# Holding the next weight slabs until the input tiles are in, copying the rotary tables across partitions on GpSimd, and three smaller edits in a hybrid encoder layer

## The reference

```python
h = rms_norm(x, norm_mix_pre)
u_pool, q, k, v, g_pool, g_attn = split(h @ w_in)          # 512, 1536, 1536, 1536, 1024, 1024
y_pool = pool_mixer(u_pool, w_pool_grp, pool_scale) @ w_pool_br   # 4 groups, centred means minus self
q, k = apply_rope(q, cos, sin), apply_rope(k, cos, sin)
o, lse = dilated_window_attention(q, k, v, dilation, 64)   # 3 head groups: dilation 1, 4, 16
y_attn = merge(o, lse) @ w_attn_br
x = x + rms_norm((sigmoid(g_pool) * y_pool + sigmoid(g_attn) * y_attn) @ w_out, norm_mix_post)
h2 = rms_norm(x, norm_ffn_pre)
x = x + rms_norm((silu(h2 @ w_ffn_gate) * (h2 @ w_ffn_up)) @ w_ffn_down, norm_ffn_post)
```

## Time and profile before

| | us |
|---|---|
| median of 3 runs (lowest, highest) | 1183.47 (1183.24, 1185.29) |
| the profiled execution | 1180.95 |
| its span on the slowest core | 1179.4 |
| spans of the other cores | 1174.4 to 1179.4 |
| PE busy in the span | 1086.2 (92%) |
| DVE, ACT, POOL busy | 538.1, 461.7, 86.3 |

### The profile page before, as it was taken

One profiled execution on the slowest core, in us unless ns is written; L12 is line 12 of the kernel. 1 busy time (PEld: TensorE's weight loads), 2 busy tenths in 40 slices (PEclk: granted clock), 3 DMA queues, 4 the chain that ended last, 5 costly groups with the idle time before them and its releaser, 6 DMA issues.

```text
span 1179.4 us, 19451 instructions; the slowest of 8 cores (1174.4 to 1179.4 us)
## 1 busy us (share of the span) xinstructions
PE 1086.2 (92%) x6781; PEld 591.4 (50%) x6896; DVE 538.1 (46%) x823; ACT 461.7 (39%) x882; POOL 86.3 (7%) x173
## 2 busy tenths in 40 slices
PE   2689989799999899999999999999999999999995
PEld 1456746455776487444444444444444444444442
DVE  3464485796548867334434867412121221222331
ACT  3453455565555555622222877411111111112211
POOL 6210000000000000001000000111111010000000
PEclk9799999999999999999999999999999999999998
DMA  8951210112021302623301842355544220333321
GB/s 190 229 135 28 37 28 11 19 21 44 10 43 22 64 11 38 126 39 57 49 1 54 262 151 106 54 82 83 82 76 73 36 36 1 108 108 107 108 90 54
DMA packets 32399, 84.62 MB, mean 72 GB/s; under 512 B 4016, under 2 KB 4272, under 8 KB 32176
## 3 DMA queue, kind: packets, MB, share of 16 engines
q0 software_dynamic: 18768, 36.31, 19.8%
q1 hardware_dynamic: 13536, 47.06, 12.2%
HBM read 102.89 MB, written 16.78 MB: 101 GB/s over the span
## 4 chain that ended last, share of the span: by engine, by line
PE 77%; DVE 7%; ACT 6%; DMA 5%; issue 4%; ACTq 0%; DVEq 0%; SPq 0%; POOL 0%; POOLq 0%
PE ps L173 64%; PE ps L170 12%; DMA arena<-x 5%; ACT arena L184 5%; DVE arena L187 2%; DVE arena L190 2%; DVE arena L201 2%; ACT arena L255 0%; DVE arena L197 0%; DVE ps L187 0%; DVE arena L195 0%; PE ps L176 0%; ACTq L68 0%; DVEq L68 0%; ACT L255 0%
## 5 line engine op out<-in xcount | busy, mean ns | idle before, releaser
L173 PE MATMUL ps<-arena 128*128 128x512 bf16 (+2 forms) x4196 | 916.2, 368 | 26.9 <-DVE arena L201 15.5
L173 PEld LDWEIGHTS ps<-arena 128*128 128x128 bf16 x4304 | 410.9, 98 | 487.6 <-issue 39.3
L184 ACT ACTIVATE arena<-ps 128x512 bf16<-128x512 f32 (+5 forms) x556 | 339.6, 619 | 633.9 <-PE ps L173 517.4
L187 DVE TENSOR_TENSOR arena<-ps,arena 128x512 bf16<-128x512 f32 (+3 forms) x332 | 223.8, 677 | 426.5 <-PE ps L173 318.0
L170 PE MATMUL ps<-arena 128*128 128x256 bf16 (+4 forms) x2329 | 223.9, 240 | 10.6 <-DVE arena L201 8.5
L170 PEld LDWEIGHTS ps<-arena 128*128 128x128 bf16 x2336 | 169.8, 105 | 35.0 <-issue 14.4
L187 DVE TENSOR_TENSOR arena<-arena 128x512 bf16<-128x512 bf16 (+2 forms) x208 | 108.5, 525 | 69.3 <-ACT arena L184 60.1
L184 ACT ACTIVATE arena<-arena 128x1 f32<-128x1 f32 (+3 forms) x161 | 86.1, 538 | 59.5 <-DMA arena<-x 31.7
L190 DVE SCALAR_TENSOR_TENSOR arena<-arena 128x1024 bf16<-128x1024 f32 (+2 forms) x49 | 61.6, 1259 | 43.0 <-ACT arena L184 26.1
L187 DVE TENSOR_TENSOR ps<-ps,arena 128x512 f32<-128x512 f32 x96 | 67.2, 700 | 10.7 <-DVE arena L187 0.9
L176 PE MATMUL ps<-arena 128*128 128x128 bf16 x256 | 22.3, 238 | 42.0 <-DVE arena L190 41.7
(11 more groups left out here) (24 smaller groups left out, 86.4 us busy)
## 6 DMA issues: line engine op xcount, KB each, us to landing
arena<-x SPq DMA_DIRECT2D x32, 512.0 KB, 6.0
y<-arena SPq DMA_DIRECT2D x31, 512.0 KB, 2.9
arena<-y SPq DMA_DIRECT2D x16, 512.0 KB, 4.1
arena<-w_qk POOLq DMA_DIRECT2D x24, 256.0 KB, 3.9
arena<-w_fg POOLq DMA_DIRECT2D x22, 256.0 KB, 5.1
arena<-w_fu POOLq DMA_DIRECT2D x22, 256.0 KB, 5.0
arena<-w_fd POOLq DMA_DIRECT2D x11, 512.0 KB, 7.6
arena<-w_gt POOLq DMA_DIRECT2D x16, 256.0 KB, 4.0
```

The source lines that it names most:

```text
L173: tk.op("pe", lambda e: e.matmul(out, lhsT=lhsT, rhs=rhs, start=start, stop=stop), reads, writes, mark)
L184: tk.op("act", lambda e: e.activation(out=out, in_=in_, func=func, **kw), reads, writes)
L187: tk.op(eng, lambda e: e.tensor_tensor(out=out, in0=in0, in1=in1, op=op), reads, writes)
```

## The change

Four things are changed.

1. Loads. SP lets three tiles of `x` be under way instead of two. The tables come as one load of 32 partitions (512 KB in all instead of 2 MB), issued after tile 3; POOL copies them to partitions 32 to 63 and then 64 to 127, in four quarters, eight copies of 1024 words per partition. The copies stand on POOL behind `issue_qk(0)` and ahead of the memsets. `issue_v(1)`, `issue_qk(1)`, the memsets of slots 2 and 3, `issue_qk(2)`, `w_pgrp` and `issue_qk(3)` come after a wait for tile 14.
2. Key halves. The two copies of a key step write two resources instead of one; every user of a query/key slot lists them through `qk_res`.
3. Pooled half steps. `u_step` works in two halves with a bank and a copy of 256 columns each. For groups 2 and 3 the `band_step` of the group before is put between the halves; the four gate steps stand between the steps of the last group instead of behind all of them.
4. Drain order in the `p4` stage. Tiles 0 to 7 use three bank pairs, the third being (6,7). From t = 16 on, `fin` comes after the six stages instead of ahead of them.

```diff
-            if i in (4, 7, 10, 13):
-                q_ = (i - 4) // 3
-                DMA("sp", "c4%d" % q_, f32v(O_CS + q_ * 1024, 1024), c_cs[:, q_ * 1024:(q_ + 1) * 1024], writes=(("cs", q_),))
+            if i == 3:
+                DMA("sp", "c4", arena[0:32, O_CS:O_CS + 4096], c_cs, writes=tuple(("cs", q_) for q_ in range(4)))
...
-            if i >= 2:
-                tk._waits("sp", tk._deps((("xr", (i - 2) % 6),), ()))
+            if i >= 3:
+                tk._waits("sp", tk._deps((("xr", (i - 3) % 6),), ()))
...
+            def qk_res(s_):
+                return tuple(("QK", s_, m, tb) for m in range(3) for tb in range(4))
...
                         if n_ == 1 and made.get(("u", 1), 0):
-                            VCOPY(dst, src, reads=(("ps", k), ("Kz", res[1])), writes=(res,))
+                            VCOPY(dst, src, reads=(("ps", k), ("Kz", res[1])), writes=(("QK", res[1], 2, res[3]),))
                         else:
-                            ACT(dst, src, AF.Copy, reads=(("ps", k), ("Kz", res[1])), writes=(res,))
+                            ACT(dst, src, AF.Copy, reads=(("ps", k), ("Kz", res[1])), writes=(("QK", res[1], res[2] + n_, res[3]),))
...
-            def u_step(g, q):
+            def u_step(g, q, mid=lambda: ()):
...
+                for h_ in range(2):
+                    k = pbank()
+                    for j in range(2):
+                        i = 4 * q + 2 * h_ + j
+                        for c in range(8):
+                            MM(bank(k)[:, j * 128:(j + 1) * 128], hT[:, c, i * 128:(i + 1) * 128],
...
+                    VCOPY(u2[g % 2][:, i:i + 2, :], bank(k)[:, 0:256].rearrange("p (i f) -> p i f", i=2), reads=(("ps", k),),
+                          writes=(("u", g % 2, 2 * q + h_),))
+                    if h_ == 0:
+                        yield from mid()
+                        yield 0.25
...
             issue_qk(0)
+            for q_ in range(4):
+                for n_ in (32, 64):
+                    src = arena[0:n_, O_CS + q_ * 1024:O_CS + (q_ + 1) * 1024]
+                    dst = arena[n_:2 * n_, O_CS + q_ * 1024:O_CS + (q_ + 1) * 1024]
+                    tk.op("pool", lambda e, o_=dst, i_=src: e.tensor_copy(out=o_, in_=i_), (("cs", q_),), (("cs", q_), "pms"))
             vones(1)
             kzero(1)
...
-                if t == 10:
+                if t == 15:
+                    tk._waits("pool", tk._deps((("xr", 14 % 6),), ()))
                     issue_v(1)
                     issue_qk(1)
-                if t == 13:
+                    kzero(2)
+                    kzero(3)
+                    issue_qk(2)
                     for g in range(4):
                         DMA("pool", "w7", wgrp[g], w_pgrp[g * 128:(g + 1) * 128, :], writes=(("wgrp", g),))
                     tk.lastw["wgrp"] = ("w7", tk.cnt["w7"])
-                    issue_qk(2)
-                    kzero(2)
                     issue_qk(3)
-                    kzero(3)
...
                     addp(134, 1000, pj(grp_step, g - 1, tb), 1.0)
-                    addp(134, 1000, pj(band_step, g, tb), 2.0)
                     if g < 3:
-                        addp(134, 1000, pj(u_step, g + 1, tb), 8.0)
+                        addp(134, 1000, pj(u_step, g + 1, tb, pj(band_step, g, tb)), 10.0)
+                    else:
+                        addp(149, 1000, pj(g_step, tb, False), 8.0)
+                        addp(134, 1000, pj(band_step, g, tb), 2.0)
             for tb in range(4):
                 addp(134, 1000, pj(grp_step, 3, tb), 1.0)
-            for n in range(4):
-                addp(149, 1001, pj(g_step, n, False), 8.0)
...
             def p4_s1(i):
                 sl = i % 3
-                kb = (i % 2) * 2
+                kb = (0, 2, 6)[i % 3] if i < 8 else (i % 2) * 2
...
-                if fin[0]:
+                if fin[0] and t < NT:
                     fin[0]()
                     fin[0] = None
                 for stg, fn in reversed(list(enumerate((p4_s1, p4_s2, p4_s3, p4_s4, p4_s5, p4_s6)))):
                     if 0 <= t - stg < NT:
                         fn(t - stg)
+                if fin[0]:
+                    fin[0]()
+                    fin[0] = None
```

More of the change, by code:

```diff
@@ L143, in build_program @@
     w_fd = din("w_fd", (DFF, D))
[L144 removed]
+    c_cs = din("c_cs", (32, 4096))
     c_pk = din("c_pk", (128, 1728))
@@ L511, in run @@
                 return True
-            def u_step(g, q):
+            def u_step(g, q, mid=lambda: ()):
                 if g == 0 and q == 0:
-                    tk.inherit(tuple(("u", b_, q_) for b_ in range(2) for q_ in range(4)) +
+                    tk.inherit(tuple(("u", b_, q_) for b_ in range(2) for q_ in range(8)) +
                                tuple((n_, 0, q_) for n_ in ("grp", "grpE") for q_ in range(4)),
                                tuple(("V", 2, n2) for n2 in range(8)) + (("Vone", 2),))
[L518 to L528, removed]
+                for h_ in range(2):
[4 more added lines that the diff above has]
+                            MM(bank(k)[:, j * 128:(j + 1) * 128], hT[:, c, i * 128:(i + 1) * 128],
+                               Wu[:, c, g * 128:(g + 1) * 128], start=(c == 0), stop=(c == 7), reads=("Wu", ("hT", i)),
+                               writes=(("ps", k),), mark=(c == 7 and j == 1), shared=True)
+                            if c < 7 or j < 1:
+                                yield 0.25
+                    i = 4 * q + 2 * h_
+                    VCOPY(u2[g % 2][:, i:i + 2, :], bank(k)[:, 0:256].rearrange("p (i f) -> p i f", i=2), reads=(("ps", k),),
+                          writes=(("u", g % 2, 2 * q + h_),))
+                    if h_ == 0:
+                        yield from mid()
+                        yield 0.25
                 if g == 3 and q == 3:
@@ L536, in band_step @@
                     tk.inherit(tuple((n_, 1, q_) for n_ in ("grp", "grpE") for q_ in range(4)),
-                               tuple(("QK", 0, m, q_) for m in range(2) for q_ in range(4)) + (("Kz", 0),))
+                               qk_res(0) + (("Kz", 0),))
                 k = pbank()
@@ L552, in band_step @@
                         MM(bank(k)[:, j * 128 + a:j * 128 + b], u2[g % 2][:, i + e, :], bg[:, o_:o_ + b - a], start=(e == 0),
-                           stop=(n_ == len(parts) - 1), reads=(("u", g % 2, (i + e) // 4), "C1b"), writes=(("ps", k),),
+                           stop=(n_ == len(parts) - 1), reads=(("u", g % 2, (i + e) // 2), "C1b"), writes=(("ps", k),),
                            mark=(j == 3 and n_ == len(parts) - 1), shared=True)
@@ L636, in emit_S @@
                 W = 512 // len(tl)
-                qk = tuple(("QK", slot, m, tb) for m in range(2) for tb in range(4))
+                qk = qk_res(slot)
                 need(("u", jp * 3 + g), i)
@@ L752, in g_step @@
                 if n == 0:
-                    tk.inherit(tuple(("sg", q_) for q_ in range(6)), tuple(("QK", 1, m, q_) for m in range(2) for q_ in range(4)))
+                    tk.inherit(tuple(("sg", q_) for q_ in range(6)), qk_res(1))
                 if n == 6:
-                    tk.inherit(tuple(("sg", q_) for q_ in (6, 7)), tuple(("QK", 2, m, q_) for m in range(2) for q_ in range(4)))
+                    tk.inherit(tuple(("sg", q_) for q_ in (6, 7)), qk_res(2))
                 k = pbank()
@@ L826, in _rest @@
                 if i == 122:
-                    tk.inherit(("Wab",), tuple(("QK", 0, m, tb) for m in range(2) for tb in range(4)))
+                    tk.inherit(("Wab",), qk_res(0))
                     DMA("pool", "w9", Wab, w_abr.rearrange("(j p) d -> p j d", p=128), writes=("Wab",))
@@ L872, in _rest @@
                     if dc == 4:
[L873 removed]
+                        tk.inherit((("fr", 6), ("fr", 7)), tuple((n_, 1, q_) for n_ in ("grp", "grpE") for q_ in range(4)) + qk_res(0))
                         tk.inherit(tuple(("fr", i) for i in range(6)),
[L875 removed]
+                                   qk_res(3))
                     if dc >= 4:
```

8 lines of the change are left out of this document (3 added, 5 removed).

## The result

The changed kernel takes 1168.75 us (median of four executions, 1166.61 to 1169.98) beside 1184.06 us for the kernel before on the same chip: a ratio of 0.9868, 95% interval 0.9850 to 0.9886, about 15.6 us faster. I had said 1161 us, range 1154 to 1171. The direction and the range hold; some 7 of the 22.7 us are missing. The profiled execution took 1169.98 us (span 1168.5 us, core 1; the other seven cores end between 1160.0 and 1164.6).

The account below looks back on a forecast made before the run. PE bounds most of the span; the room is at the start, where early slabs take half the bandwidth while x is late. Loads 15.8 + key halves 0 + pooled 2.2 + drain 4.7 = 22.7 us, giving 1161 us, range 1154 to 1171.

Parts of the forecast that it names:

- rival A: Opening: POOL's table copies get in the way of DVE's scaling, 9 us lost; 13.7 us gain in all, 1169.8 us; chance 0.10.
- Pooled half steps: Attention, 430 to 482 us: PE's waits for `u_step` copies and at the list's end shrink; 2.2 us gain, bounds 3.8 and -0.5.
- new bank waits: Pooled half steps: 0.3 us taken off their gain for PE waiting anew for banks.
- Loads: Opening: with slabs held and tables cut, x comes sooner; tile 15 starts 15.8 us earlier, ends 11.0 and 18.5 us.
- Rival E: Opening: HBM with all cores reading, not the slabs, holds x up; only 6.9 us remain, 1176.6 us; chance 0.08.
- what is late next: Opening, after the loads: the tile pipeline itself, DVE about 2.5 us a tile; pitch taken as 2.75 us.
- rival B: Opening: every x wait after tile 1 goes, 21.2 us; 28.1 us in all, 1155.4 us; chance 0.12.
- Holding costs nothing: Opening: second value slab, held for tile 14, is issued at 45 us and lands 8 us ahead of need; cost nothing.
- Rival C: Opening: held slabs behind POOL's copies come too late, slower; 1189.6 us at 7 us a copy; chance 0.06.
- Copies: Opening: POOL's eight table copies take 1.8 us each, 14.4 us, from about 21 to 36 us, with no loss counted.
- Key halves: Key steps: splitting the resource gains 0, since the PSUM bank entry still makes the second copy wait for the first.
- Drain: `p4` stage: 0.2 us at the start, 6.0 less a new 1.25 us wait at the end; 4.7 us, bounds 3 and 6.

Follow-up runs that it names:

- halves_late: Changed kernel with the pooled features of groups 0 and 1 computed in whole steps as before, half steps only for groups 2 and 3; 1161.08 us, ratio 0.9798.
- best_sq: Changed kernel without pooled half steps, key copies side by side, and ACT's squares of the next tile queued ahead of evacuations; 1154.88 us, ratio 0.9746.
- tables_late: Changed kernel with the table load behind x tile 6 instead of 3 and POOL's copies behind its second memsets; 1169.47 us, ratio 0.9884.
- no_pool: Changed kernel without the pooled half steps and with the gate steps back at the end; 1165.68 us, ratio 0.9839.
- drain_only: Kernel before with only the third bank pair and the stages ahead of the block's rest in `p4`; ratio 0.9963, 4.4 us faster.
- keys_free: Kernel before with two resources per key step and its two copies not entered as PSUM bank writers, so read side by side; ratio 0.9908, 10.9 us faster.
- pool_only: Kernel before with only the pooled half steps, band step between halves, and gate steps moved between the last group's steps; ratio 1.0037, 4.4 us slower.

## Why the prediction was right, and where it was wrong

The direction is right by mechanism, and the time lies in the range, but partly by luck. The 1155 to 1167 us that I gave to the forecast by itself doesn't hold the measured time, nor does its upper end follow from the bounds of the parts, which add up to 1170 us (11.0 - 0.5 + 3 = 13.5 us of gain). The range reached to 1171 us to take in rival A (1169.8 us), which hardly happened; it was wide enough for another mistake of the same size. By the parts as measured alone, 6.6 of the missing 7.1 us are the pooled half steps (4.4 us slower instead of 2.2 faster) 1.7 the loads and 0.3 the drain; the key halves give 1.1 back, which their interval doesn't tell from nothing.

**Pooled half steps: the step that failed.** I counted -2.2 us, bounds -3.8 and +0.5; the part measured alone is +4.4 us. I read the waits of one stretch, 430 to 482 us, where a band step and a `grp_step` stand between the uses of a bank, and gave the half steps the same neighbours everywhere. The steps of group 0 stand at 350 to 415 us directly between key steps: there a half needs a second of the three banks while a key step holds it for two serial copies. Two pairs of waits of 1.31 + 1.63 us came in, each in the place of a wait of 0.42 us: 2 x 2.52 = 5.0 us. Against them stand the waits that did go at the end of the list, less those that came there; some 3.6 us of waits are left, and 1.6 us of lower clock, for which I had no term. The cost I had named, 0.3 us for "new bank waits", had no row behind it; the row was the earlier trace rows, the second key copy that waits 1.01 us for ACT, and I used it for the key halves only. `halves_late` shows that the sign turns with the place. Of the gain in the good place, 1.1 us are in the trace, at the end of the list less than I said, for with the gate steps gone from there a wait of 1.64 us stands bare, and the clock is lower behind it.

**Loads: mechanism right, size some 2 us too large.** 15.8 us forecast; 14.1 us for the part alone (11.0 to 17.2, so 15.8 is not excluded), 13.5 us at the first reload on the mean of the cores, 10.3 on core 1. Rival E (1176.6 us) is out by the hold alone: 12.7 us. On core 1 both factors of the step were optimistic: tile 4 at 26.56 instead of 23.5 us, for tile 1 waited 6.96 us for x, and the pitch 2.91 us ((58.62 - 26.56) / 11) instead of 2.75. (On the mean of the cores tile 4 comes 1.4 us earlier, at 22.06 instead of 23.42 us, and the pitch is 2.83 us.) The pitch has a cause that I hadn't listed under "what is late next": ACT's squares queue behind evacuations that wait for PE. `best_sq` shows that this cause costs nothing in the end, since PE's own work has become the bound; for the same reason rival B would hardly have come true with all waits for x gone, though no run took them all away. Of the marks I had set, ACT's waits for x (near 11 us; 16.9) and tile 15 (51 to 58 us; 58.62, with the other cores between 50.03 and 54.49) were missed by little on this core.

**Holding costs nothing: right.** The slab is issued at 48.39 us (45 forecast) and PE starts on it at 71.92 us with no wait. Rival C is out with it.

**Copies: right, and the table later than said.** 1.55 us a copy on the mean where I took 1.8; on core 1 the first four take 1.03 us each and the last four, beside which DVE scales tiles, 1.84 to 1.86. The table landed at 25.04 us, not 21: 17.7 us from issue to use. By the Trainium skill (SBUF — State Buffer, "Door 1: The DMA port swizzle") I had estimated 2.8 us for that load alone by half of the ports; the row cannot tell ports from the queue that it shared with x. `tables_late` shows that no time hung on it. Rival A is nearly out: the four scalings of tiles that stand on DVE beside POOL's copies lost 1.2 us in all against the 1.28 us of the earlier trace rows, where rival A needed 9. The timeline of DVE, and the fourth and fifth copy on POOL:

```profile
28.49 2.14 DVE L190 SCALAR_TENSOR_TENSOR arena<-arena 128x1024 bf16<-128x1024 f32 x1 [3.08 <-ACT arena L184]
...
31.15 1.45 DVE L190 SCALAR_TENSOR_TENSOR arena<-arena 128x1024 bf16<-128x1024 f32 x1
...
33.31 1.28 DVE L190 SCALAR_TENSOR_TENSOR arena<-arena 128x1024 bf16<-128x1024 f32 x1
...
35.14 1.43 DVE L190 SCALAR_TENSOR_TENSOR arena<-arena 128x1024 bf16<-128x1024 f32 x1
...
28.52 1.03 POOL L593 COPY arena<-arena 64x1024 f32<-64x1024 f32 x1
29.68 1.84 POOL L593 COPY arena<-arena 32x1024 f32<-32x1024 f32 x1
```

By the Trainium skill (SBUF — State Buffer, "Who interferes with whom") the two exclude each other for a whole instruction; the rows agree. The scaling at 28.49 us ends 1.07 us after the copy that began beside it, with 2.14 us instead of 1.28, and the next copy, which begins while it runs, takes 1.84 us instead of 1.03. What I had wrong was who loses: the last four copies lost 0.8 us each, 3.3 us in all, on POOL, which then waited 5.16 us for x anyway.

**Key halves: right.** 0 forecast, no change measured, and for the reason given: the bank's entry in `Tracker.op` still orders the copies. Over the span of the changed kernel PE's waits for them are 14.9 us, beside 15.3 in the earlier trace rows:

```profile
PE ps L173 <- DVE arena L201: 14.9, 16, 1.7
```

I said that freeing the second copy could pay and didn't price it; it is 10.9 us.

**Drain: right.** 4.7 us forecast, 4.4 us alone (2.7 to 5.9). The waits of PE in the changed kernel from 637 to 743 us, and the rows of its start and end, for the earlier trace rows:

```profile
PE ps L176 <- ACT arena L184: 0.9, 3, 0.3
PE ps L176 <- DVE arena L190: 0.8, 1, 0.8
PE ps L173 <- DVE arena L187: 0.5, 1, 0.5
```

```profile
647.20 0.61 PE L176 MATMUL ps<-arena 128*128 128x128 bf16 x8 [0.77 <-DVE arena L190]
...
659.69 0.61 PE L176 MATMUL ps<-arena 128*128 128x128 bf16 x8 [0.28 <-ACT arena L184]
...
728.83 3.61 PE L173 MATMUL ps<-arena 128*128 128x512 bf16 x16 [0.50 <-DVE arena L187]
732.28 0.61 PE L176 MATMUL ps<-arena 128*128 128x128 bf16 x8
```

The 1.87 us at the start are gone and come back as three waits for ACT of 0.28 to 0.31 us and one of 0.77 for DVE, as said: the lead goes back to ACT. At the end the new wait for the bank pair is there, 0.50 us where I said 1.25, and transposes and matmuls run at 0.61 and 3.61 us again instead of 0.96 and 4.98. The stretch from the gates to the end of `p4` is 6.28 us shorter in the trace of core 1, 1.6 us more than the sum; 0.9 us of that belongs to the pooled part (without it the stretch takes 262.85 us in `no_pool` and 262.84 in `drain_only`, 5.4 less than before), and the rest is open.

## What to carry to other kernels

Before a step is split to free a bank sooner, look at which steps stand beside it in the order of issue and how long they hold the other banks: the same split gains between short steps and loses between steps with two serial evacuations. And look at what the moved steps leave behind: the gate steps had covered the waits at the end of the list, and without them these stand bare. Where several steps wait for one bank, shortening its evacuation (two engines reading it side by side, each its own 64 partitions) was worth ten times what the half steps gave in their good place (10.9 us beside about 1). And a prefetch that isn't due for 20 us could be held here until the critical stream was in, at no cost; the condition is that the time to its first use is longer than its own landing.

## What the runs showed of the hardware

- ScalarE and VectorE read one PSUM bank side by side, each half of its partitions, at the durations that they have one after the other (0.69 us for DVE's copy); that alone is worth 10.9 us here. One such pair in the timeline of `keys_free`:

```profile
413.31 0.69 DVE L403 CAST arena<-ps 64x512 bf16<-64x512 f32 x1 [0.33 <-PE ps L170]
...
413.30 0.59 ACT L406 ACTIVATE arena<-ps 64x512 bf16<-64x512 f32 x1
```

- Behind two waits of TensorE close together, of 1.64 and 0.44 us or of 1.31 and 1.63 us, stood 10 us with a mean granted clock of 0.83, so in part at the lower of its two levels (1.2 and 2.4 GHz). The first pair has it on four of the eight cores of the changed kernel and on five of `halves_late`, the second on five of the changed kernel, with the same instructions on all. One such fall cost some 1.6 us of attention (409.0, 410.4 to 410.7 and 412.2 us with none, one and two in `pool_only`).
- VectorE's scaling, which reads two SBUF tensors, and GpSimd's copy hold each other up: 1.28 and 1.03 us alone, up to 2.14 and 1.86 us beside each other.
- The eight cores come to the same tile at different times with the same program: tile 15 between 50.03 and 58.62 us in the changed kernel. The one that came last set the time of the profiled execution.
